# Local attention heads of a hybrid decoder step: the next key is rotated in banks of its own, during the head before

## The chip, the cores and the metric

The kernel runs on one core of one Trainium2 chip. The metric is the device time of one execution in microseconds (us), here the median over several executions. A profiled execution is one such execution, recorded by the hardware profiler; its span is the time from its first to its last recorded instruction. The engines of the core are called TensorE (PE in the rows, its weight loads PEld), VectorE (DVE), ScalarE (ACT), GpSimd (POOL) and SyncE (SP).

## What is computed

One inference step of a four-layer decoder for 512 prompt rows and 8 sample rows, which go through the layers together as 520 columns. The third layer is a sparse attention with 8 heads of 128 dimensions. Cut to what matters:

```python
def dsa_prompt(x, w_in, w_out):
    q, k, v, qi, ki, wi = dsa_project(x, pos, w_in)     # x @ w_in, then rope on q, k, qi, ki
    idx, valid = indexer_topk(qi, wi, ki, pos, n_top)   # 128 keys for each query
    s = einsum('bqhd,bqkhd->bqhk', q, k[idx]) * ATTN_HEAD_DIM ** -0.5
    p = softmax(where(valid, s, -inf))
    o = einsum('bqhk,bqkhd->bqhd', p, v[idx])
    return o @ w_out, k, v, ki                          # rotated keys and values are outputs too
```

The sample rows attend to a paged cache, in a stage after the heads.

## The kernel before

All engines run one program each, ordered by semaphores; a table counts what each stage adds to each semaphore, so that a wait names a semaphore and a count. Matmul operands in f32 are split into a rounded high half and a low half (the difference), and a product is three matmuls: high by high, high by low, low by high.

Weights come in units of 1024 x 128. A unit is loaded by SP into one of four raw slots, ScalarE writes its high half (`split_hi`, line 440), VectorE its low half (`split_lo`, line 450), and TensorE multiplies it with all 520 columns (`multiply`, line 466): 8 chunks of 6 matmuls, 260 columns each. `split_next` (line 458) splits the unit two ahead, once the product that used the same half buffers is done. SP loads the unit four ahead after the low half of a unit is written.

The head stage (`attend`, lines 1032 for ScalarE, 1585 for VectorE, 2148 for TensorE) goes through 8 heads in order, two in each pass of a loop. Each head has a key unit and a value unit. The projection of the next units lies between the softmax steps of a head: four pieces, each ahead of one of the four score tiles. PSUM has eight banks: 0 to 3 hold the projections, 4 to 7 the four score tiles, their transposes, and more:

- rotation of the key: `rotate` (line 2059) multiplies the raw key with an exchange matrix into banks 4 and 5; `d_rotate` (line 1488, three VectorE operations) makes the rotated key from it.
- transposes of the rotated key (bank 6) and of the raw value (bank 7), with their 8 sample rows in banks 4 and 5; ScalarE copies them out (lines 1052 to 1057), GpSimd stores them (lines 715, 717).
- scores of tile t in bank 4 + t; VectorE adds the bias and takes the maximum (line 1650), ScalarE exponentiates (line 1061), VectorE normalises (line 1661); TensorE transposes the weights back into bank 4 + t (line 1821), ScalarE and VectorE split them (lines 1084 and 1722).
- output, four tiles of value products, all in bank 4 (`output`, three matmuls, lines 527 to 529); ScalarE and VectorE write its two halves (lines 1068 and 1667).

In heads 0 to 5 VectorE also does two steps of a top-8 search in each softmax tile (`select`, line 1591), and in head 6 it works out rows of the cache (`find_rows`, line 1605). The stage after the heads (`past`, lines 735, 1070, 1670, 2223) starts gathers from the cache when the last head's line 1667 is done.

In each head ScalarE issues in this order: key copy, split, rounding of the query, value copy, split, rounding of the key (line 1049), the copies of lines 1052 to 1057, four exponentials with the rounding of the transposed weights one tile behind, output. VectorE: low half of weights, query (line 1627), rotation, low half of the key (line 1633), low half of weights, low half of the value (line 1638), four softmax tiles, output. TensorE: rotation, second half of the value's projection, transposes, scores, softmax tiles with projections and value products.

## Time and profile before

| | |
|---|---|
| runs | median 3302.01 us of 3 (3300.86 to 3304.73) |
| profiled execution | 3304.24 us, span 3302.6 us |
| busy, share of the span | TensorE 3095.8 us (94%), weight loads 2918.9 (88%), VectorE 1569.0 (48%), ScalarE 1042.5 (32%), GpSimd 209.5 (6%) |
| chain that ended last | TensorE 87%, VectorE 8%, ScalarE 3%, issue 2% |
| granted TensorE clock | mean 0.957 |
| head stage | about 1604 to 1826 us of the span |

The shares of busy time are averages over stages. The chain is followed back from the last instruction; "issue" is time in which an engine waited for nothing that the profile shows. The granted clock is a share of full speed, and each moment has one of two levels, 1.2 or 2.4 GHz.

### The profile page before, as it was taken

What the parts mean: (1) busy time and instruction counts of PE and PEld (TensorE: products, weight loads), DVE (VectorE), ACT (ScalarE), POOL (GpSimd) and SP (SyncE); (2) the same over time, 40 slices, a digit from 0 to 9 for tenths busy, and PEclk for the clock granted to TensorE, in tenths of its full rate; (3) what the DMA queues carried; (4) which work ended last, traced back from release to release, by engine and by line L of the source; (5) the groups of instructions that cost most, each with busy time, mean ns of one, the idle gap of its engine ahead of it and who ended that gap; (6) DMA issues with size and microseconds to landing.
All of it is one profiled execution on the core that took longest, in us unless ns stands there. A gap on an engine that the chain in (4) does not pass through costs nothing.

```text
span 3302.6 us, 55336 instructions
## 1 busy us (share of the span) xinstructions
PE 3095.8 (94%) x23519; PEld 2918.9 (88%) x23519; DVE 1569.0 (48%) x2426; ACT 1042.5 (32%) x1459; POOL 209.5 (6%) x342
## 2 busy tenths in 40 slices
PE   8999998999976999998887899999999999799997
PEld 7898896999976999986777799999989989699996
DVE  4555555332357332357865453234555555533234
ACT  3333332422234322233333143122523333332223
POOL 0111111000000000010001100000021011000000
PEclk9999998999987999999898899999999999899998
DMA  6344333232311332321122323233344433333231
GB/s 147 131 133 157 128 116 125 77 112 74 98 56 54 89 103 83 96 64 51 52 59 71 116 76 99 84 92 92 94 150 124 146 131 115 109 90 105 75 101 40
DMA packets 491333, 323.14 MB, mean 98 GB/s; under 512 B 29179, under 2 KB 467707, under 8 KB 491130
## 3 DMA queue, kind: packets, MB, share of 16 engines
q1 hardware_dynamic: 464338, 230.14, 24.4%
q0 software_dynamic: 26800, 90.18, 7.9%
q8 instruction: 150, 2.46, 0.3%
q14 instruction: 45, 0.37, 0.0%
HBM read 275.90 MB, written 44.82 MB: 97 GB/s over the span
## 4 chain that ended last, share of the span: by engine, by line
PE 87%; DVE 8%; ACT 3%; issue 2%; DMA 0%; POOL 0%; SPq 0%; ACTq 0%; DVEq 0%; POOLq 0%
PE ps L477 71%; PE ps L1821 2%; PE ps L527 2%; PE ps L529 2%; PE ps L528 2%; PE ps L1951 2%; PE ps L508 2%; PE ps L1941 1%; DVE wf L1537 1%; DVE tiny L1535 1%; DVE wf L1761 1%; DVE wf L1786 1%; DVE w_l L454 1%; PE ps L2309 1%; PE ps L2062 1%
## 5 line engine op out<-in xcount | busy, mean ns | idle before, releaser
L477 PE MATMUL ps<-x_h,w_h 128*128 128x260 f32 x4576 | 942.1, 287 | 8.8 <-DVE w_l L454 6.6
L477 PE MATMUL ps<-x_h,w_l 128*128 128x260 f32 x4576 | 928.4, 285 | 0.0
L477 PE MATMUL ps<-x_l,w_h 128*128 128x260 f32 x4576 | 927.5, 285 | 0.0
L454 DVE TENSOR_TENSOR w_l<-w_raw,w_h 128x1024 fp32r<-128x1024 f32 (+3 forms) x440 | 527.8, 1200 | 796.8 <-ACT w_h L448 796.2
L477 PEld LDWEIGHTS ps<-x_h,w_h 128*128 128x128 f32 x4576 | 715.9, 191 | 32.8 <-issue 23.7
L448 ACT ACTIVATE w_h<-w_raw 128x1024 fp32r<-128x1024 f32 (+3 forms) x440 | 456.0, 1036 | 904.9 <-PE ps L477 874.3
L477 PEld LDWEIGHTS ps<-x_h,w_l 128*128 128x128 f32 x4576 | 712.4, 190 | 0.0
L477 PEld LDWEIGHTS ps<-x_l,w_h 128*128 128x128 f32 x4576 | 712.0, 190 | 0.0
L477 PE MATMUL ps<-rr,w_h 128*128 128x260 f32 x3968 | 639.3, 283 | 2.2 <-DVE w_l L454 1.1
L477 PEld LDWEIGHTS ps<-rr,w_h 128*128 128x128 f32 x3968 | 543.4, 188 | 4.0 <-issue 3.0
L477 PE MATMUL ps<-rr,w_l 128*128 128x260 f32 x1984 | 399.4, 283 | 0.0
L477 PEld LDWEIGHTS ps<-rr,w_l 128*128 128x128 f32 x1984 | 306.7, 189 | 0.0
L1733 DVE TENSOR_TENSOR wf<-ps,wf 128x520 f32<-128x520 f32 x88 | 61.5, 699 | 248.5 <-PE ps L477 248.5
L1091 ACT ACTIVATE wf<-ps 128x520 f32<-128x520 f32 x88 | 53.4, 606 | 337.5 <-PE ps L477 334.6
L527 PE MATMUL ps<-rr 128*128 128x512 f32 (+5 forms) x332 | 121.9, 370 | 18.3 <-DVE rr L1633 10.4
L1821 PE MATMUL ps<-ident,wf 128*128 128x128 f32 (+4 forms) x607 | 95.2, 291 | 32.5 <-DMA wf<-in_x_sample 9.8
L1747 DVE SCALAR_TENSOR_TENSOR x<-x,ps 128x520 f32<-128x520 f32 x40 | 27.8, 696 | 196.1 <-PE ps L477 196.1
L1821 PEld LDWEIGHTS ps<-ident,wf 128*128 128x128 f32 (+4 forms) x607 | 70.5, 142 | 55.7 <-issue 30.8
L529 PE MATMUL ps<-rr 128*128 128x512 f32 (+5 forms) x332 | 116.2, 352 | 0.0
L528 PE MATMUL ps<-rr 128*128 128x512 f32 (+5 forms) x332 | 116.1, 351 | 0.0
L1304 DVE SCALAR_TENSOR_TENSOR wf<-ps,wf 128x512 f32<-128x512 f32 x128 | 89.8, 743 | 17.8 <-PE ps L1942 14.5
L527 PEld LDWEIGHTS ps<-rr 128*128 128x128 f32 (+1 forms) x332 | 64.7, 196 | 35.7 <-issue 19.4
(272 smaller groups left out, 2772.7 us busy)
## 6 DMA issues: line engine op xcount, KB each, us to landing
w_raw<-in_ffn_w_in SPq DMA_DIRECT2D x176, 512.0 KB, 3.8
w_raw<-in_ret_w_in SPq DMA_DIRECT2D x96, 512.0 KB, 4.0
out<-wf POOLq DMA_DIRECT2D x72, 512.0 KB, 3.3
wf<-in_state_ret POOLq DMA_DIRECT2D x64, 512.0 KB, 5.7
w_raw<-in_ffn_w_out SPq DMA_DIRECT2D x32, 768.0 KB, 4.7
w_raw<-in_ffn_w_out SPq DMA_DIRECT2D x32, 640.0 KB, 4.2
w_raw<-in_ret_w_out SPq DMA_DIRECT2D x64, 256.0 KB, 2.9
w_raw<-in_dsa_w_in SPq DMA_DIRECT2D x27, 512.0 KB, 3.9
```

The lines of the kernel that those rows point to most:

```text
L448: C.activation(whole(stage, k, w_h[:, n % 2, 0:m]), landed(stage, k, n, m), ACT.Copy).then_inc(S["w_hi"], 1)
L454: V.tensor_tensor(whole(stage, k, w_l[:, n % 2, 0:m]), landed(stage, k, n, m), whole(stage, k, w_h[:, n % 2, 0:m].bitcast(F32)), ALU.subtr ...
L477: mm = M.matmul(ps[:, 2 * (n % 2) + b, 0:HALF], lhs[:, c, :], rhs[:, c, cols], start=(c == 0 and term == 0), stop=(c == cs - 1 and term == 2))
L508: mm = M.matmul(ps[:, 2 * n + b, 0:HALF], lhs, rhs[:, c, cols], start=(c == 0 and term == 0), stop=(c == DC - 1 and term == 2))
L527: M.matmul(out, lhs_h, rhs_h, start=start, stop=False)
L528: M.matmul(out, lhs_h, rhs_l, start=False, stop=False)
L529: return M.matmul(out, lhs_l, rhs_h, start=False, stop=stop)
L1091: C.activation(halves(sil[:, q]), acc[0], ACT.Silu).then_inc(S["sil"], 1)
L1304: V.scalar_tensor_tensor(st[:, b % 4, d], ps[:, 7, :], k_f[:, d, SEQ + b:SEQ + b + 1], st[:, b % 4, d], ALU.mult, ALU.add).then_inc(S["s_n ...
L1733: V.tensor_tensor(halves(h_raw[:, q]), acc[1], halves(sil[:, q]), ALU.mult).then_inc(S["h_raw"], 1)
L1821: return M.transpose(out, src, ident[0:n, 0:n])
L1951: mm = M.matmul(ps[32 * j:32 * j + 4, 6, :], qz[:, i % 2, d, g, j, :], st[:, (2 * g + j) % 4, d, :], start=(g + d == 0), stop=(g == NB // ...
```

## The change

The loop over passes and halves becomes one loop over heads `g`; all its steps are the same, in another order and with other waits:

- TensorE rotates the key of head g + 1 into banks 5 and 6 (before: 4 and 5), in head g, after the transpose of the fourth weight tile and ahead of the third and fourth value products, once the low half of the third tile is written. Head 0's key is rotated ahead of the loop.
- ScalarE copies the raw key of head g + 1 and splits the next unit behind the third exponential of head g (before: after the output of head g); the query of head g + 1 is rounded behind the fourth weight tile. The rounded key goes ahead of the value copy. The copies of the 8 sample rows go ahead of the large copies of the same bank.
- VectorE splits the low half of that unit ahead of the fourth weight tile's low half, and does the rotation and the query of head g + 1 ahead of the output's low half.
- TensorE's waits follow: the key's transposes no longer wait for the last weight tile, the 8-row key transpose waits for line 1667, the first and second score wait for the 8-row copies alone, the third for the key copy, the fourth for the value's low half, as before.

No operation is added or taken away. The core of the diff:

```diff
@@ ScalarE, attend
+    def key_row(g):
+        at, q = marks.here(stage, g // 2), g % 2
+        act.wait_ge(*at("d_rope", 3 * q))
+        d_copy(at, 0, stage, g // 2, 2 * q, 0)
+        split_next(split_hi, act, stage, g // 2, 2 * q)
+    def query(g):
+        at, q = marks.here(stage, g // 2), g % 2
+        act.wait_ge(*at("s_mm", 4 * q))
+        C.activation(qa_h.rearrange("p (o t) -> p o t", o=1), q_h[:, g:g + 1, :], ACT.Copy).then_inc(S["qa_h"], 1)
+    key_row(0)
+    query(0)
+    for g in range(2 * n):
+        i, q = g // 2, g % 2
+        act.wait_ge(*at("d_rope", 3 * q + 3))
+        act.wait_ge(*at("s_mm", 4 * q))
+        C.activation(ka_h, d_f[:, 0], ACT.Copy).then_inc(S["k_hi"], 1)
+        act.wait_ge(*at("vv_tp", q))
+        d_copy(at, 1, stage, i, 2 * q + 1, 1)
+        split_next(split_hi, act, stage, i, 2 * q + 1)
+        act.wait_ge(*at("kv_out", 64 * q))
+        act.wait_ge(*at("kk_tp", q + 1))
+        C.activation(kvs[0:NB, 0], ps[0:NB, 4, 0:P], ACT.Copy).then_inc(S["kn_cp"], 1)
+        C.activation(kn, view(ps[:, 6], 0, QT, P), ACT.Copy).then_inc(S["kn_cp"], 1)
+        act.wait_ge(*at("vv_tp", q + 1))
+        C.activation(kvs[0:NB, 1], ps[0:NB, 5, 0:P], ACT.Copy).then_inc(S["vn_cp"], 1)
+        C.activation(va_h, view(ps[:, 7], 0, QT, P), ACT.Copy).then_inc(S["vv_hi"], 1)
+        C.activation(vn, view(ps[:, 7], 0, QT, P), ACT.Copy).then_inc(S["vn_cp"], 1)
+        for t in range(QT):
+            w, m = (t + 1) * P, 4 * q + t
+            act.wait_ge(*at("nmx", m + 1))
+            C.activation(pe_[:, t % 2, 0:w], pe_[:, t % 2, 0:w], ACT.Exp, bias=dnm[:, t:t + 1],
+                         accum_out=dsm[:, t:t + 1]).then_inc(S["p_exp"], 1)
+            if t:
+                p_hi(at, m - 1, t - 1)
+            if g < 2 * n - 1 and t == 2:
+                key_row(g + 1)
+        p_hi(at, 4 * q + 3, 3)
+        if g < 2 * n - 1:
+            query(g + 1)
+        act.wait_ge(*at("pv", q + 1))
+        C.activation(o_h[:, g:g + 1, 0:SEQ], ps[:, 4:5, :], ACT.Copy).then_inc(S["o_hi"], 1)
@@ VectorE
-def d_rotate(at, k, tab, slot, to):
+def d_rotate(at, k, tab, slot, to, bank=4):
-    V.tensor_tensor(halves(d_t), ps[:, 4:6, 0:HALF], halves(tab[:, 1]), ALU.mult).then_inc(S["d_rope"], 1)
+    V.tensor_tensor(halves(d_t), ps[:, bank:bank + 2, 0:HALF], halves(tab[:, 1]), ALU.mult).then_inc(S["d_rope"], 1)
@@ VectorE, attend
+    def key_row(g):
+        at, q = marks.here(stage, g // 2), g % 2
+        dve.wait_ge(*at("k_hi", q))
+        dve.wait_ge(*at("kk_tp", q))
+        d_rotate(at, q, dtab, 0, 0, 5)
+    def query(g):
+        at, q = marks.here(stage, g // 2), g % 2
+        dve.wait_ge(*at("qa_h", q + 1))
+        dve.wait_ge(*at("s_mm", 4 * q))
+        V.tensor_copy(qa_l.rearrange("p (o t) -> p o t", o=1), q_l[:, g:g + 1, :].bitcast(F32)
+                      ).then_inc(S["qa_l"], 1)
+    split_next(split_lo, dve, stage, 0, 0)
+    query(0)
+    key_row(0)
+    for g in range(2 * n):
+        i, q = g // 2, g % 2
+        dve.wait_ge(*at("d_rope", 3 * q + 3))
+        V.tensor_copy(ks_d[:, g:g + 1], d_f[:, 0:1, SEQ:T]).then_inc(S["ks_cp"], 1)
+        dve.wait_ge(*at("k_hi", q + 1))
+        V.tensor_tensor(ka_l, d_f[:, 0], ka_h.bitcast(F32), ALU.subtract).then_inc(S["k_lo"], 1)
+        split_next(split_lo, dve, stage, i, 2 * q + 1)
+        dve.wait_ge(*at("d_raw", 2 * q + 2))
+        V.tensor_copy(vs_d[:, g:g + 1], d_raw[:, 1:2, SEQ:T]).then_inc(S["ks_cp"], 1)
+        dve.wait_ge(*at("vn_cp", 2 * q + 2))
...
+        if g < 2 * n - 1:
+            split_next(split_lo, dve, stage, (g + 1) // 2, 2 * ((g + 1) % 2))
+        p_lo(at, 4 * q + 3, 3)
+        if g < 2 * n - 1:
+            key_row(g + 1)
+            query(g + 1)
+        dve.wait_ge(*at("o_hi", q + 1))
+        V.tensor_tensor(o_l[:, g:g + 1, 0:SEQ], ps[:, 4:5, :], o_h[:, g:g + 1, 0:SEQ].bitcast(F32), ALU.subtract
+                        ).then_inc(S["o_lo"], 1)
@@ TensorE
-def rotate(at, k, m, slot):
+def rotate(at, k, m, slot, bank=4):
-        mm = M.matmul(ps[:, 4 + b, 0:HALF], m, d_raw[:, slot, cols], start=True, stop=True)
+        mm = M.matmul(ps[:, bank + b, 0:HALF], m, d_raw[:, slot, cols], start=True, stop=True)
@@ TensorE, attend
+    def key_row(g):
+        at, q = marks.here(stage, g // 2), g % 2
+        pe.wait_ge(*at("d_raw", 2 * q + 1))
+        rotate(at, q, rotm, 0, 5)
+    pe.wait_ge(*late("sc_cp", 0))
+    key_row(0)
+    for g in range(2 * n):
+        i, q = g // 2, g % 2
+        multiply(pe, stage, i, 2 * q + 1, x_h, x_l, DC, range(4, 8))
+        pe.wait_ge(*at("d_rope", 3 * q + 3))
+        for t in range(QT):
+            turn(ps[:, 6, t * P:(t + 1) * P], d_f[:, 0, t * P:(t + 1) * P], P)
+        pe.wait_ge(*at("o_lo", q))
+        turn(ps[0:NB, 4, 0:P], d_f[:, 0, SEQ:T], P).then_inc(S["kk_tp"], 1)
+        pe.wait_ge(*at("d_raw", 2 * q + 2))
+        pe.wait_ge(*at("p_lo", 4 * q))
+        for t in range(QT):
+            turn(ps[:, 7, t * P:(t + 1) * P], d_raw[:, 1, t * P:(t + 1) * P], P)
+        turn(ps[0:NB, 5, 0:P], d_raw[:, 1, SEQ:T], P).then_inc(S["vv_tp"], 1)
+        pe.wait_ge(*at("qa_l", q + 1))
+        pe.wait_ge(*at("k_lo", q + 1))
+        for t in range(QT):
+            w, tile = (t + 1) * P, slice(t * P, (t + 1) * P)
+            if t == 0:
+                pe.wait_ge(*at("kn_cp", 2 * q + 1))
+            elif t == 1:
+                pe.wait_ge(*at("vn_cp", 2 * q + 1))
+            elif t == 2:
+                pe.wait_ge(*at("kn_cp", 2 * q + 2))
+            elif t == 3:
+                pe.wait_ge(*at("vv_lo", q + 1))
+                if g == 6:
+                    pe.wait_ge(*late("row", 10))
+                    turn(ps[:, 7, 0:NB], row, NB).then_inc(S["row_t"], 1)
+                    pe.wait_ge(*late("row_c", 1))
+            three(ps[:, 4 + t, 0:w], qa_h[:, tile], qa_l[:, tile], ka_h[:, 0:w], ka_l[:, 0:w]
+                  ).then_inc(S["s_mm"], 1)
+        for t in range(QT):
+            m = 4 * q + t
+            if g < 2 * n - 1:
+                multiply(pe, stage, (g + 1) // 2, 2 * ((g + 1) % 2) + pieces[t][0], x_h, x_l, DC, pieces[t][1])
+            pe.wait_ge(*at("p_n", m + 1))
+            for j in range(t + 1):
+                mm = turn(ps[:, 4 + t, j * P:(j + 1) * P], pe_[:, t % 2, j * P:(j + 1) * P], P)
+            mm.then_inc(S["p_tp"], 1)
+            if t == 3 and g < 2 * n - 1:
+                pe.wait_ge(*at("p_lo", m))
+                key_row(g + 1)
+            if t:
+                output(at, m - 1, t - 1)
+        output(at, 4 * q + 3, 3).then_inc(S["pv"], 1)
```

## Rows read from the trace of the kernel before

**Rows 1.** Busy time by stretch, head stage: width us, busy (instructions), PEclk, DMA share, GB/s.

```profile
1636.47:1661.55 25.08, 20.91 (x162) 19.51 (x160) 17.80 (x47) 10.63 (x24) 2.57 (x4) 1.00 0.19 51
1661.55:1690.89 29.34, 25.23 (x164) 23.80 (x165) 18.58 (x51) 10.63 (x24) 2.58 (x4) 0.83 0.23 66
...
1773.04:1804.98 31.94, 24.97 (x166) 22.96 (x164) 16.03 (x46) 10.63 (x24) 4.62 (x6) 0.84 0.28 84
1804.98:1824.78 19.80, 15.00 (x70) 13.08 (x69) 9.32 (x30) 8.43 (x21) 2.67 (x4) 0.62 0.19 54
1636.47:1773.04 136.57, 115.86 (x812) 108.73 (x811) 90.90 (x242) 53.16 (x120) 12.88 (x20) 0.90 0.21 59
```

**Rows 2.** Waits, 1628 to 1800 us: engine line <- waited for: us, times, longest.

```profile
PE ps L2062 <- DVE rr L1667: 11.0, 7, 1.6
```

**Rows 3.** Timeline of TensorE: start, us, line, operation [idle before <- releaser].

```profile
1693.90 0.30 PE L527 MATMUL ps<-rr 128*128 128x128 f32 x1 [1.48 <-DVE rr L1633]
...
1694.86 0.39 PE L527 MATMUL ps<-rr 128*128 128x256 f32 x1 [0.44 <-ACT wf L1057]
...
1696.54 0.40 PE L477 MATMUL ps<-x_h,w_h 128*128 128x260 f32 x2
...
1708.86 0.33 PE L527 MATMUL ps<-rr 128*128 128x128 f32 x1 [0.46 <-DVE rr L1722]
...
1710.14 0.28 PE L529 MATMUL ps<-rr 128*128 128x128 f32 x1
1711.98 1.11 PE L2062 MATMUL ps<-wf 128*128 128x260 f32 x4 [1.56 <-DVE rr L1667]
1712.74 0.59 PE L477 MATMUL ps<-x_h,w_h 128*128 128x260 f32 x2
```

**Rows 4.** The same view of ScalarE, 1676 to 1697 us.

```profile
1676.68 0.72 ACT L1061 ACTIVATE wf<-wf,tiny 128x512 f32<-128x512 f32 x1 [1.29 <-DVE tiny L1654]
...
1690.99 0.60 ACT L971 ACTIVATE wf<-ps 128x520 f32<-128x520 f32 x1 [5.74 <-PE ps L477]
1691.49 1.05 ACT L448 ACTIVATE w_h<-w_raw 128x1024 fp32r<-128x1024 f32 x1
1692.44 0.63 ACT L1049 ACTIVATE rr<-wf 128x520 fp32r<-128x520 f32 x1
1692.96 0.59 ACT L1052 ACTIVATE wf<-ps 128x512 f32<-128x512 f32 x1
1693.44 0.25 ACT L1053 ACTIVATE wf<-ps 8x128 f32<-8x128 f32 x1
1693.60 0.57 ACT L1055 ACTIVATE rr<-ps 128x512 fp32r<-128x512 f32 x1
```

**Rows 5.** The same view of VectorE, 1640 to 1697 us.

```profile
1641.10 0.28 DVE L1650 CUSTOM_DVE_ANT_0 wf<-ps,wf 128x128 f32<-128x128 f32 x1
...
1651.89 0.55 DVE L1722 TENSOR_TENSOR rr<-ps,rr 128x384 fp32r<-128x384 f32 x1
...
1680.29 0.69 DVE L1722 TENSOR_TENSOR rr<-ps,rr 128x512 fp32r<-128x512 f32 x1 [1.15 <-ACT rr L1084]
...
1684.75 1.23 DVE L454 TENSOR_TENSOR w_l<-w_raw,w_h 128x1024 fp32r<-128x1024 f32 x1 [0.75 <-ACT w_h L448]
1685.89 0.42 DVE L1627 CAST rr<-rr 128x520 fp32r<-128x520 f32 x1
1686.26 0.70 DVE L1492 TENSOR_TENSOR wf<-ps,wf 128x520 f32<-128x520 f32 x1
...
1688.34 0.17 DVE L1631 COPY wf<-wf 128x8 f32<-128x8 f32 x1
...
1694.92 0.68 DVE L1638 TENSOR_TENSOR rr<-ps,rr 128x512 fp32r<-128x512 f32 x1
```

**Rows 6.** The same view of TensorE, at the first hand-over.

```profile
1629.89 2.07 PE L2062 MATMUL ps<-wf 128*128 128x260 f32 x4 [1.56 <-DVE rr L1667]
1631.40 1.00 PE L477 MATMUL ps<-x_h,w_h 128*128 128x260 f32 x2
```

More of the change, by code:

```diff
@@ new lines, in attend @@
+                split_next(split_lo, dve, stage, 0, 0)
[3 more added lines that the diff above has]
+                    i, q = g // 2, g % 2
+                    at = marks.here(stage, i)
+                    dve.wait_ge(*at("d_rope", 3 * q + 3))
[6 more added lines that the diff above has]
+                    dve.wait_ge(*at("vn_cp", 2 * q + 2))
+                    V.tensor_tensor(va_l, view(ps[:, 7], 0, QT, P), va_h.bitcast(F32), ALU.subtract
+                                    ).then_inc(S["vv_lo"], 1)
+                    if g == 6:
+                        find_rows()
+                        dve.wait_ge(*late("row_t", 1))
+                        V.tensor_copy(rows.bitcast(U32), ps[:, 7, 0:NB]).then_inc(S["row_c"], 1)
+                    for t in range(QT):
+                        w, m, to = (t + 1) * P, 4 * q + t, BIAS_AT[t]
+                        dve.wait_ge(*at("s_mm", m + 1))
+                        if t >= 2:
+                            dve.wait_ge(*at("p_tp", m - 1))
+                        carry(dve)
+                        V.tensor_tensor_reduce(out=pe_[:, t % 2, 0:w], in0=ps[:, 4 + t, 0:w], in1=bias[:, to:to + w],
+                                               scale=ASCALE, scalar=-3.0e38, op0=ALU.add, op1=ALU.max,
+                                               accum_out=dmx[:, t:t + 1]).then_inc(S["s_sc"], 1)
+                        dve.wait_ge(*at("s_sc", m + 1))
+                        V.tensor_scalar(dnm[:, t:t + 1], dmx[:, t:t + 1], -1.0, None, ALU.mult).then_inc(S["nmx"], 1)
+                        if g < 6:
+                            select(2 * (4 * g + t))
+                            select(2 * (4 * g + t) + 1)
+                        dve.wait_ge(*at("p_exp", m + 1))
+                        V.reciprocal(drc[:, t:t + 1], dsm[:, t:t + 1]).then_inc(S["p_rc"], 1)
+                        dve.wait_ge(*at("p_rc", m + 1))
+                        V.tensor_scalar(pe_[:, t % 2, 0:w], pe_[:, t % 2, 0:w], drc[:, t:t + 1], None, ALU.mult
+                                        ).then_inc(S["p_n"], 1)
+                        if t:
+                            p_lo(at, m - 1, t - 1)
+                    if g < 2 * n - 1:
[7 more added lines that the diff above has]
+                                    ).then_inc(S["o_lo"], 1)
@@ new lines, in key_row @@
+                def key_row(g):
[6 more added lines that the diff above has]
+                    i, q = g // 2, g % 2
+                    at = marks.here(stage, i)
+                    multiply(pe, stage, i, 2 * q + 1, x_h, x_l, DC, range(4, 8))
[21 more added lines that the diff above has]
+                            pe.wait_ge(*at("vv_lo", q + 1))
+                            if g == 6:
+                                pe.wait_ge(*late("row", 10))
[3 more added lines that the diff above has]
+                              ).then_inc(S["s_mm"], 1)
+                    for t in range(QT):
+                        m = 4 * q + t
[8 more added lines that the diff above has]
+                            key_row(g + 1)
+                        if t:
+                            output(at, m - 1, t - 1)
+                    output(at, 4 * q + 3, 3).then_inc(S["pv"], 1)
```

125 lines of the change are left out of this document (removed).

## The prediction

> **What bounds the kernel now.** I read three views of the head stage (lines 1032, 1585 and 2148), about 1604 to 1826 us of the span. First the busy time by stretch [rows 1], cut at the end of each head's V product; I call that moment M. A head takes 25.08 us where TensorE's granted clock is 1.00 throughout, and 29.34 us where it is 0.83; the two kinds alternate, and five heads take 136.57 us at a mean of 0.90. TensorE is busy 20.91 of 25.08 us, VectorE 17.80, ScalarE 10.63: TensorE is the bound, but it stands still some 4 us a head, and then runs partly at 1.2 GHz. Second, the list of what TensorE waits for [rows 2]: the largest item is the rotation's matmul (line 2062) waiting for the low half of the previous head's output (line 1667), 1.6 us at every one of seven hand-overs. Third, the same waits in order of time for one head at full clock [rows 3]: 1.48 us before the first score, for the low half of the key (line 1633), 0.44 before the second, 0.46 inside the value products, 1.56 before the rotation. ScalarE's rows [rows 4] say why the scores wait: V copy, weight rounding, key rounding, key copy and value copies stand one behind the other from M + 0.10.
>
> **The change, part by part.** All at full clock, from rows 3 to 5, M = 1690.89.
>
> *Rotation in banks 5 and 6, ahead of the last two value products.* Now the rotation writes banks 4 and 5, and bank 4 holds the output, so it must wait until the output is read. The last output matmul is issued at 1710.14; the next could follow 0.11 later, as within the products, at 1710.25. From there to the start of the V product at 1712.74 pass 2.49 us [rows 3]. With the rotation gone from there, the V product follows at once: -2.49. The rotation itself is not saved; it costs 1712.74 - 1711.98 = +0.76 between the fourth transpose and the third product. There it fills the time in which the fourth product waits for its low half: the 0.46 us wait with some 0.15 us of restart, -0.6. Net -2.33 a hand-over. It needs the K copy (ScalarE, after the third exponential) and the low half of tile 2; both end before the fourth transpose.
>
> *K copy and weight split behind the third exponential.* ScalarE issues the pair in 1692.44 - 1690.99 = 1.45 us [rows 4]. It moves into a stretch where ScalarE stood idle 1.29 us before the fourth exponential [rows 4], so that exponential can be later by 0.2 us; were nothing idle, by 1.45. I take 0 for TensorE, since VectorE has two top-8 steps to do meanwhile, and TensorE has no wait for the normalised weights (line 1661) in the steady heads; cover gone, it is 0.2 a head. On VectorE the weights' low half goes ahead of the last tile's low half, where VectorE idles 1.15 us [rows 5]; the subtraction issues in 1685.89 - 1684.75 = 1.14. 0. The loads on SP's queue follow the low half, so they start earlier; none was waited for. The POOL queue keeps its order.
>
> *Rotation on VectorE ahead of the output's low half.* Three operations, 1688.34 - 1686.26 = 2.08 us, and the query cast, 0.37 us [rows 5], now stand between the last low half and line 1667. Behind them wait the key's transposes (after the V product, 3.07 us long) and the 8-row transpose into bank 4. I follow VectorE from M: value low half done at 4.0 (below); the four softmax tiles take 1651.89 + 0.55 - 1641.10 = 11.3, to 15.3; split and last low half to 17.2, rotated key at 19.3, output's low half at about 20.3. The next M is at 22.0. So 1.7 to 2.7 us are spare, and the cost is 0; if the spare is used up, every further us is one a head.
>
> *Key rounded ahead of the value copy, small copies first.* The key is ready long before M, so its rounding leaves the chain behind M. Then, with issue times of [rows 4], the 8-row key copy goes at M + 1.55 where the rounding stood, the key copy at 1.70, the 8-row value copy at 2.18, value rounding at 2.33, value copy (as long as the key copy) at 2.81, done at 3.4. The value's low half (0.60 us, line 1638) ends at 4.0 instead of 4.63 (1694.92 + 0.60) [rows 5], and the fourth score, which waits for it, releases the next projection at M + 4.9 instead of 1696.54 - 1690.89 = 5.65 [rows 3]: -0.75. In these 4.9 us TensorE has four short waits, none over 0.7 us by the same times.
>
> A rule stands against stopping there. TensorE's busy row counts 20.91 us in the full-clock head, its weight-load row 19.51 [rows 1]. The Trainium skill (Perfetto Trace Analysis, Identifying the Most-Contended Engine) says that matmul busy time is no good measure of TensorE's headroom and that the weight loads' busy share is a good one. By that rule a head could shrink to an estimated 19.5 us, and the time would be some 12 us lower than mine. No row shows work that would fill those last waits, so the sum stays with the waits that the edits remove.
>
> **The sum.** A full-clock head: 25.08 - 2.33 - 0.75 = 22.0. Five heads: 136.57 - 110 = 26.6 if all run at full clock. What the clock keeps costing is not shown, so I bound it: nothing at best; at worst as much as now, 136.57 - 5 x 25.1 = 11.1 us. In the trace the clock fell to 1.2 GHz after the 1.56 us stop before the rotation, or after the 1.48 and 0.44 us stops in the scores; the longest stop left is about 0.7 us. I take 2.5 us, near the lower end. The first hand-over ran at 1.2: rotation 1.51 us and V product 1636.47 - 1631.40 = 5.07 [rows 6] instead of 0.76 and 3.07, so it gives 2.33 + 2.75 = 5.1. The last (inside 31.94 us at 0.84 [rows 1]) gives 2.33, 0.75 for the score chain, through which the row search starts earlier, and 0 to 2.75 for the clock; I take 1.4: 4.5. The eighth head (19.80 us) has no projections under it and follows the ScalarE and VectorE chain: 0.7. Sum: 26.6 - 2.5 + 5.1 + 4.5 + 0.7 = 34.4 us. The stage after the heads starts its gathers on the last line 1667, so all of it moves to the end. The profiled execution took 3304.24 us: 3269.8. It stands 2.2 us over the median of 3302.01, so the prediction for a median is 3268.
>
> **Rivals.**
> (1) The clock gains nothing: the shorter waits still let it fall as often. For it: a third of the time of every second head is at 1.2 GHz although no stop there exceeds 1.6 us [rows 1, 3]. Against: the large stops go. Gain 26.6 - 11.1 + 2.3 + 3.1 + 0.7 = 21.6: about 3280.
> (2) VectorE becomes the bound. It is busy 17.80 us in a head of 25.08 [rows 1] and would be in one of 22.0, with rotation and cast in series ahead of line 1667. If its waits on ScalarE (1.15 and 2 to 3 us more in a head) stay where they are, it overruns its spare by some 1.6 us: 5 x 1.6 = 8 us back, 3276.
> (3) Slower: TensorE stays at 1.2 GHz through the heads. Place: the stretch from M to the fourth score, now transposes and short scores with four stops. Of the 22.0 us, 16.9 are matmul; at half speed throughout a head would take 38.9 instead of 27.3, seven hand-overs +81 us: 3383. It decides from 10.6 us at 1.2 GHz in a head (5.3 us lost). For it: the eighth head, without wide projections, has 0.62 over 19.80 us [rows 1]. Against: each steady head has wide projections for over half its time, during which the clock came back in the trace.
> (4) The edits do nothing that counts: the wait before the rotation only moves to the 8-row transpose into bank 4, which now waits for line 1667. For it, that line comes 0.1 us later; against, 3.07 us of V product lie before it. 3302, within the bound.
>
> **How the numbers follow.** Forecast 0.70, rival 1 0.15, rival 2 0.08, rival 3 0.03, rival 4 0.04. A measurement of this kernel tells 0.2% (6.6 us) from no change. Forecast and rivals 1 and 2 are faster by more: 0.93; rival 4 the same: 0.04; rival 3 slower: 0.03. The best case has no fall of the clock left and a full 2.75 at the last hand-over, 38.3 us: 3264; a few us more if later stages keep the clock better. The other end takes in rivals 1 and 2 with both their bounds: 3284. Range 3260 to 3284.
>
> **What would show it.** Right: M to M of 22 to 23 us, granted clock near 1.00 in these stretches, no wait of line 2062 for line 1667, the first score waiting for the 8-row key copy and the fourth for line 1638, V product directly behind the value products. Wrong: a new wait of TensorE for the rotated key or for line 1661, stretches with 0.83 as often as now, or a time over 3284.

## The result, and the profile after

The changed kernel takes 3270.47 us, the median of 4 runs (3267.33 to 3272.78), the kernel before 3303.37 (3300.86 to 3308.75, 4 runs): a ratio of 0.9899, 95% interval 0.9887 to 0.9911. The profiled execution took 3270.22 us, its span is 3268.5 us (before: 3304.24 and 3302.6), and the mean granted clock rose from 0.957 to 0.962. The time was predicted at 3268. That it came so close is luck: two errors of the prediction cancel in it, as the stages show.

The head stage by stretch, from M to M as in [rows 1]: width, busy time (instructions) of TensorE, its weight loads, VectorE, ScalarE and GpSimd, then PEclk, DMA share, GB/s. The first line is one head; the lines behind the mark are the sum of five heads, then head 6 and head 7.

```profile
1629.73:1651.73 22.00, 20.82 (x165) 19.57 (x163) 18.08 (x48) 10.53 (x24) 2.58 (x4) 1.00 0.26 73
...
1629.73:1739.73 110.00, 104.07 (x813) 97.78 (x811) 90.22 (x242) 52.65 (x120) 12.90 (x20) 1.00 0.25 73
1739.73:1766.91 27.18, 23.06 (x166) 21.58 (x164) 15.70 (x46) 10.53 (x24) 4.62 (x6) 0.87 0.32 98
1766.91:1786.06 19.15, 13.94 (x70) 11.93 (x68) 8.82 (x29) 7.91 (x20) 2.67 (x4) 0.72 0.18 55
```

The alternation of [rows 1] is gone: each of five heads takes 22.00 us at a granted clock of 1.00, 110.00 us where there were 136.57. TensorE's busy time in a full-clock head is as before (20.82 us beside 20.91); only its idle time went. Of the 26.57 us that the five heads give, 14.78 are idle time of TensorE and 11.79 busy time, which was longer at the lower clock (115.86 us busy before, 104.07 after).

What TensorE waits for, 1628 to 1770 us, answers to [rows 2]: us in total, times, longest.

```profile
PE ps L1849 <- DVE wf L1630: 3.2, 1, 3.2
PE ps L527 <- ACT wf L1060: 2.9, 7, 0.4
PE ps L527 <- DVE rr L1661: 2.7, 5, 0.5
PE ps L1849 <- ACT wf L971: 1.5, 7, 0.2
PE ps L527 <- DVE wf L1666: 0.3, 1, 0.3
```

The 11.0 us ahead of the rotation are gone, and the rotation (now line 2090) is in no wait. What is left per head is 0.21, 0.42 and 0.54 us, on the copies and on the value's low half behind M. The 3.2 us are the row search of head 6.

TensorE in order of time, one head, which answers to [rows 3]:

```profile
1645.03 0.60 PE L1849 MATMUL ps<-ident,wf 128*128 128x128 f32 x4
1645.46 1.04 PE L2090 MATMUL ps<-wf 128*128 128x260 f32 x4
1646.15 0.41 PE L527 MATMUL ps<-rr 128*128 128x128 f32 x1
...
1648.53 0.28 PE L529 MATMUL ps<-rr 128*128 128x128 f32 x1
1648.64 0.46 PE L477 MATMUL ps<-x_h,w_h 128*128 128x260 f32 x2
...
1653.67 0.30 PE L527 MATMUL ps<-rr 128*128 128x128 f32 x1 [0.42 <-ACT wf L1060]
...
1655.90 0.50 PE L527 MATMUL ps<-rr 128*128 128x512 f32 x1 [0.54 <-DVE rr L1661]
...
1656.70 0.40 PE L477 MATMUL ps<-x_h,w_h 128*128 128x260 f32 x2
```

The rotation takes 1646.15 - 1645.46 = 0.69 us between the fourth transpose and the third product. The V product starts 0.11 us behind the last value product, where 2.60 us lay (1712.74 - 1710.14 in [rows 3]). From M (1651.73) to the next projection piece pass 4.97 us, where 5.65 passed.

ScalarE in the same head, which answers to [rows 4]: key copy and split run where it stood idle, and the exponential (line 1069) follows without a gap.

```profile
1641.28 0.60 ACT L971 ACTIVATE wf<-ps 128x520 f32<-128x520 f32 x1
1641.77 1.06 ACT L448 ACTIVATE w_h<-w_raw 128x1024 fp32r<-128x1024 f32 x1
1642.71 0.72 ACT L1069 ACTIVATE wf<-wf,tiny 128x512 f32<-128x512 f32 x1
```

The last head's output comes 38.7 us earlier than before, yet the end only 34.0 us (3304.24 - 3270.22). The other 4.7 us are lost in stages that the change does not touch. One piece of them lies in the cache stage, first before, then after:

```profile
1844.78:1869.10 24.32, 18.98 (x52) 7.33 (x52) 4.43 (x12) 0.49 (x2) 2.33 (x3) 0.86 0.24 74
```

```profile
1806.06:1832.06 26.00, 20.38 (x52) 8.32 (x52) 4.71 (x12) 0.49 (x2) 2.64 (x3) 0.77 0.25 79
```

The same 52 matmuls take 1.7 us more, at 0.77 in place of 0.86.

### The profile page after: what moved, and what is told of

Same layout as the page of the kernel before. It is cut to its first block, busy times and chain, and to the rows that moved or that the text cites. A ratio compares the mean times of both kernels' runs of the same rounds, so it can differ in the third digit from the quotient of the medians.

```text
span 3268.5 us, 55344 instructions
## 1 busy us (share of the span) xinstructions
PE 3081.4 (94%) x23519; PEld 2905.9 (89%) x23519; DVE 1568.0 (48%) x2426; ACT 1041.5 (32%) x1459; POOL 209.6 (6%) x342
## 4 chain that ended last, share of the span: by engine, by line
PE 88%; DVE 7%; ACT 3%; issue 2%; DMA 0%; POOL 0%; SPq 0%; ACTq 0%; DVEq 0%; POOLq 0%
PE ps L477 71%; PE ps L1849 2%; PE ps L527 2%; PE ps L528 2%; PE ps L529 2%; PE ps L1979 2%; PE ps L508 2%; PE ps L1969 1%; DVE wf L1548 1%; DVE wf L1789 1%; DVE tiny L1546 1%; DVE wf L1814 1%; DVE w_l L454 1%; ACT w_h L448 1%; PE ps L2346 1%
## 5 line engine op out<-in xcount | busy, mean ns | idle before, releaser
L477 PEld LDWEIGHTS ps<-x_h,w_h 128*128 128x128 f32 x4576 | 710.6, 190 | 32.2 <-issue 23.7
L1849 PE MATMUL ps<-ident,wf 128*128 128x128 f32 (+4 forms) x607 | 95.3, 290 | 34.6 <-DMA wf<-in_x_sample 9.9
L1849 PEld LDWEIGHTS ps<-ident,wf 128*128 128x128 f32 (+4 forms) x607 | 70.3, 142 | 57.9 <-issue 31.5
L527 PEld LDWEIGHTS ps<-rr 128*128 128x128 f32 (+1 forms) x332 | 64.1, 194 | 26.0 <-issue 11.9
```

The costliest lines, as they stand in the source:

```text
L477: mm = M.matmul(ps[:, 2 * (n % 2) + b, 0:HALF], lhs[:, c, :], rhs[:, c, cols], start=(c == 0 and term == 0), stop=(c == cs - 1 and term == 2))
L527: M.matmul(out, lhs_h, rhs_h, start=start, stop=False)
L1849: return M.transpose(out, src, ident[0:n, 0:n])
```

## The experiments

Each run leaves a profile. Five heads are measured from one output copy to the sixth; by that measure they take 136.60 us at a clock of 0.90 before and 110.00 at 1.00 after. The lead is how much earlier than in the profile of before a point is reached.

**1. The score chain undone.** In the changed kernel ScalarE rounds the key behind the value copy again, the large copies go first, and scores 0 and 1 wait for both copies of their pair.

```diff
-act.wait_ge(*at("d_rope", 3 * q + 3))
-act.wait_ge(*at("s_mm", 4 * q))
-C.activation(ka_h, d_f[:, 0], ACT.Copy).then_inc(S["k_hi"], 1)
 act.wait_ge(*at("vv_tp", q))
 d_copy(at, 1, stage, i, 2 * q + 1, 1)
 split_next(split_hi, act, stage, i, 2 * q + 1)
+act.wait_ge(*at("d_rope", 3 * q + 3))
+act.wait_ge(*at("s_mm", 4 * q))
+C.activation(ka_h, d_f[:, 0], ACT.Copy).then_inc(S["k_hi"], 1)
...
-    pe.wait_ge(*at("kn_cp", 2 * q + 1))
+    pe.wait_ge(*at("kn_cp", 2 * q + 2))
```

> The changed kernel with one part undone: ScalarE rounds the rotated key behind the value copy and its split again, and the first two score tiles wait for both copies of their pair again. Theory (each stop on the way from the last value product to the scores is worth its length): the five heads between heads 1 and 6 go from 22.00 to about 22.75 us each, seven hand-overs together cost about 5 us, 3275 to 3276 us against 3270 for the changed kernel; TensorE shows stops of about 1.0 us or more ahead of the first score tile. Rival 1 (it was the order on ScalarE that held the clock in the heads): the clock of the five heads falls below 0.95 and they take 24 us or more, 3280 us or above. Rival 2 (the score chain is hidden behind the K and V transposes): heads stay at 22.0 us, 3270 us.

Measured: 3279.25 us, ratio to before 0.9918 (0.9900 to 0.9935). Its five heads, then the waits that came back, then three stretches of 2 us in one head:

```profile
1627.24:1747.38 120.14, 109.51 (x813) 104.12 (x812) 90.28 (x243) 52.62 (x120) 12.87 (x20) 0.93 0.24 67
...
1680.60:1682.60 2.00, 0.55 (x4) 0.44 (x4) 1.79 (x3) 1.92 (x6) 0.59 (x1) 0.89 0.00 0
1682.60:1684.60 2.00, 2.00 (x7) 2.00 (x8) 1.93 (x9) 0.49 (x2) 1.99 (x4) 0.50 0.60 139
1684.60:1686.60 2.00, 2.00 (x12) 1.73 (x12) 1.93 (x8) 0.56 (x2) 0.00 (x0) 0.76 1.12 342
```

```profile
PE ps L527 <- DVE rr L1656: 8.9, 6, 1.5
PE ps L527 <- ACT wf L1065: 2.6, 6, 0.4
```

Rival 1, in the heads: 24.03 us each, at 0.93, and some 9 us in all. Behind the stop of 1.5 us, in which TensorE was busy 0.55 of 2 us, it runs at 1.2 GHz (0.50) through the scores that follow and into the next pieces. Of the 2.03 us a head that this part gives, 0.94 are more idle time (10.63 us in five heads, 5.93 in the changed kernel) and 1.09 longer busy time (109.51 us, 104.07), at the clock that falls behind the stop.

**2. The wait for the output's low half put back**, ahead of the V product:

```diff
+pe.wait_ge(*at("o_lo", q))
 multiply(pe, stage, i, 2 * q + 1, x_h, x_l, DC, range(4, 8))
```

> The changed kernel with one wait added: TensorE starts the second half of a head's V projection only when VectorE has written the low half of the previous head's output, which is the wait that stood ahead of the rotation before. Theory: a stop of 1.5 to 1.7 us comes back at each of seven hand-overs, from 0; at full clock a head takes 23.5 to 23.7 us, 11 to 12 us in all, 3281 to 3282 us. Rival 1 (this stop alone also lowers the granted clock, which was 0.83 to 1.00 in the heads before): the five heads show under 0.95 and take 25 us or more, 3290 us or above. Rival 2 (the stop is given back, since what follows was waiting for ScalarE and VectorE anyway): under 0.5 us a head, 3273 us or less.

Measured: 3282.38 us (0.9928, 0.9911 to 0.9944). Five heads:

```profile
1625.34:1746.19 120.85, 107.86 (x812) 100.87 (x811) 90.27 (x243) 52.59 (x120) 12.87 (x20) 0.97 0.23 67
```

For most heads the theory's mechanism: behind a stop of 1.41 us three take 23.61 to 23.62 us at 1.00, that is 1.61 more than 22.00. The other two take 25.12 and 24.88 at 0.93, as rival 1 had it for all five. So a stop at this place cost somewhat more than its length in all five heads, and the clock too in two. That the time is the theory's is partly luck: the last head's output comes 14.8 us later than in the changed kernel, and part of that comes back behind the heads (experiment 8).

**3. The rotation behind the last value product**, its own banks kept:

```diff
-if t == 3 and g < 2 * n - 1:
-    pe.wait_ge(*at("p_lo", m))
-    key_row(g + 1)
 if t:
     output(at, m - 1, t - 1)
...
 output(at, 4 * q + 3, 3).then_inc(S["pv"], 1)
+if g < 2 * n - 1:
+    key_row(g + 1)
```

> The changed kernel with TensorE's rotation of the next key behind the last value product of a head instead of ahead of the values of tile 2; its own banks are kept. Theory: the rotation then lies on the path between the last value product and VectorE's rotated key. Two matmuls cost about 0.6 us, and the rotated key (2.0 us of VectorE work) and its rounding come 2.8 us later than now, while V's second half takes about 2.9 us of TensorE: the K transposes wait little, 22.0 us a head become 22.6 to 23.5, 3274 to 3281 us. Rival (the banks alone do it, VectorE and ScalarE have spare time): 0.0 to 0.2 us a head, 3270 to 3271 us. Rival 2 (the place among the value products is what carries the gain): over 2.0 us a head, 3285 us or more.

Measured: 3269.00 us (0.9888, 0.9870 to 0.9905). Five heads and the wait that came back inside the products:

```profile
1626.27:1739.81 113.54, 105.66 (x812) 98.25 (x812) 90.17 (x242) 53.10 (x120) 12.88 (x20) 1.00 0.25 71
```

```profile
PE ps L527 <- DVE rr L1750: 2.3, 5, 0.5
```

In the heads the theory: 22.67 us or a little more each, at full clock; the place inside the products is worth 0.67 us a head, because the rotation fills the wait of 0.46 us. In the total the rival: no slower than the changed kernel. The last head's output comes 4.2 us later than in the changed kernel, and the end does not; experiment 8 takes this up.

**4. VectorE's rotation behind the output's low half:**

```diff
-if g < 2 * n - 1:
-    key_row(g + 1)
-    query(g + 1)
 dve.wait_ge(*at("o_hi", q + 1))
 V.tensor_tensor(o_l[:, g:g + 1, 0:SEQ], ...).then_inc(S["o_lo"], 1)
+if g < 2 * n - 1:
+    key_row(g + 1)
+    query(g + 1)
```

> The changed kernel with VectorE's three rotation operations and the next query's low half behind the subtraction for the output's low half instead of ahead of it. Theory: output's low half comes as early as ScalarE's copy lets it (ScalarE starts it 0.2 us behind the last value product), the rotated key about 3 us later than now, close to where the V product's second half ends; the K transposes wait 0.3 to 0.6 us a head, 3272 to 3275 us. Rival (VectorE has enough spare time that the order is worth nothing): heads stay at 22.0 us, 3270 us. Rival 2 (late query and key push the score tiles as well): over 1.0 us a head, 3278 us or more.

Measured: 3272.44 us (0.9896, 0.9879 to 0.9913), the time that the theory said, but too close to the changed kernel's 3270.47 to be told from it. The heads tell: 114.90 us for five, four of them 22.79 to 22.82 us, and one 23.66 us at a clock of 0.93. TensorE, line 1849, in one head:

```profile
1699.56 0.76 PE L1849 MATMUL ps<-ident,wf 128*128 128x128 f32 x5 [0.43 <-DVE wf L1506]
1700.72 0.77 PE L1849 MATMUL ps<-ident,wf 128*128 128x128 f32 x5 [0.40 <-ACT wf L971]
```

The key's transposes wait 0.43 us for the rotated key, and the value's 0.40 for the copy, 0.2 more than in the changed kernel. VectorE's order is worth 0.8 us a head, more than the 0.3 to 0.6 said: the rotated key ends 0.37 us behind M (1699.50 against 1699.13), where the changed kernel has it 2.6 us ahead of M, so the other order uses up the spare time.

**5. Key copy and split behind the fourth weight tile:**

```diff
-        if g < 2 * n - 1 and t == 2:
-            key_row(g + 1)
     p_hi(at, 4 * q + 3, 3)
     if g < 2 * n - 1:
+        key_row(g + 1)
         query(g + 1)
```

> The changed kernel with one part undone in the order of ScalarE: the next key's copy and the split of its weights stand behind the fourth weight tile instead of behind the third exponential. Theory: the copy then ends about 1.3 us behind the point at which TensorE wants to rotate, and VectorE's low half of the split, with the fourth weight tile's low half queued behind it, comes about 2.5 us later; a head goes from 22.0 to 24.0 to 24.8 us, 14 to 20 us in all without a loss of clock, 3284 to 3290 us. Rival 1 (the place is free, ScalarE being busy for 10.5 us of 22): under 0.3 us a head, 3272 us or less. Rival 2 (only the rotation's own wait counts, VectorE takes up the rest): 1.3 us a head, 3278 to 3281 us.

Measured: 3282.56 us (0.9923, 0.9906 to 0.9940). Five heads, and the new waits:

```profile
1630.31:1752.04 121.73, 106.22 (x813) 98.19 (x812) 90.12 (x243) 53.15 (x120) 12.88 (x20) 1.00 0.23 66
```

```profile
PE ps L2089 <- ACT wf L971: 6.4, 5, 1.3
PE ps L527 <- DVE rr L1749: 3.9, 6, 0.6
```

The theory in the heads: 24.35 us each (24.0 to 24.8 said), the rotation waiting 1.27 us for the raw key and the last product 0.65 for its low half. At the last head's output 17.5 us are lost, 1.3 of them ahead of the heads already; at the end the medians differ by 12.1, under the theory's 14 to 20, and experiment 8 shows where the rest comes back. So with own banks but without the early key copy, TensorE stops at the rotation all the same. The clock stays at 1.00, although the stops of a head (1.27 + 0.65 + 0.21 + 0.42 + 0.54 = 3.1 us) are longer than those of experiment 1 (1.48 + 0.44 + 0.21 = 2.1 us), which lowered it in every head.

**6. Own banks alone, in the kernel before:**

```diff
-pe.wait_ge(*at("o_lo", q))
-rotate(at, q, rotm, 0)
+pe.wait_ge(*late("sc_cp", 0))
+rotate(at, q, rotm, 0, 5)
...
+pe.wait_ge(*at("o_lo", q))
 turn(ps[0:NB, 4, 0:P], d_f[:, 0, SEQ:T], P).then_inc(S["kk_tp"], 1)
```

> The kernel before with one part of the change alone: the rotation writes two banks that the value products do not use, so that it no longer waits for the low half of the output, which is waited for at the 8-row transpose instead. ScalarE's key copy stays behind the output's copy. Theory: the rotation then waits for the raw key, which ScalarE copies right behind the output's copy (0.5 us later), so that only about 0.4 to 0.5 us of the stop of 11.0 / 7 = 1.57 us go; 3 to 4 us in all at the same clock, 3297 to 3304 us beside 3301 to 3311 of the kernel before. Rival (the banks are what the gain comes from): the stop is gone, 1.5 us a head and 11 us, with the clock up by some hundredths, 3290 us or less.

Measured: 3300.80 us (0.9986, 0.9977 to 0.9996). Its waits and five heads:

```profile
PE ps L527 <- DVE rr L1633: 7.1, 5, 1.5
PE ps L2062 <- ACT wf L971: 5.0, 4, 1.2
```

```profile
1625.15:1761.88 136.73, 117.59 (x811) 110.12 (x810) 90.84 (x242) 53.17 (x120) 12.88 (x20) 0.89 0.21 59
```

The theory, for the wait: the rotation now waits 1.24 us for ScalarE's key copy, in place of 1.56 for the output's low half. But the five heads take 136.73 us, as long as before (136.60), so the 0.3 us that each stop gave do not show even there.

**7. The score chain alone, in the kernel before**, the rotation untouched:

```diff
+act.wait_ge(*at("d_rope", 3 * q + 3))
+C.activation(ka_h, d_f[:, 0], ACT.Copy).then_inc(S["k_hi"], 1)
 act.wait_ge(*at("vv_tp", q))
 d_copy(at, 1, stage, i, 2 * q + 1, 1)
 split_next(split_hi, act, stage, i, 2 * q + 1)
-act.wait_ge(*at("d_rope", 3 * q + 3))
-C.activation(ka_h, d_f[:, 0], ACT.Copy).then_inc(S["k_hi"], 1)
...
-    pe.wait_ge(*at("kn_cp", 2 * q + 2))
+    pe.wait_ge(*at("kn_cp", 2 * q + 1))
```

> The kernel before with the other part of the change alone: ScalarE rounds the rotated key ahead of the value copy, copies the 8-row blocks first and releases the score tiles one by one; the rotation stays where it was, with its stop of 1.56 us. The run that undid this part in the changed kernel cost 8 us, 24.0 us a head in place of 22.0, where the part's own stop is 0.75 us: the clock fell to 0.93 in every head behind a stop of 1.48 us ahead of the first score tile. Theory (that stop, in a stretch of short transposes, is what makes the clock fall; the stop ahead of the rotation mostly does not, as the run with that stop put back showed 1.00 in four heads of five): the five heads show 24.3 to 25.0 us each at a clock of 0.97 to 1.00 in most of them, 121 to 126 us where the kernel before took 136.6; 3286 to 3295 us beside 3301 to 3310. Rival 1 (each stop is worth its length alone): 0.75 us a head, the clock between 0.83 and 1.00 from head to head as before, 3299 to 3303 us. Rival 2 (only both stops gone bring the clock back): the heads keep their mean clock of 0.90 or fall lower, 3300 us or above.

Measured: 3301.38 us (0.9990, 0.9981 to 0.9999). Five heads:

```profile
1622.56:1753.57 131.01, 114.58 (x811) 106.07 (x810) 91.62 (x242) 53.63 (x120) 12.87 (x20) 0.92 0.21 61
```

My theory fell. The stop ahead of the first score is gone (0.42 us instead of 1.48), but the clock falls in four heads of five (0.87 to 0.93). In one of them the rotation, behind its stop of 1.56 us, takes 2.07 us in place of 1.11; the fifth head stays at 1.00 with a stop of 1.57 us ahead of its rotation. The time lies in the range of rival 1 and in that of rival 2, and does not tell them apart. The theory also leaned on a misreading: in experiment 2 three heads of five stayed at 1.00, not four. In the heads the score chain alone is worth more than its time says: the five take 5.6 us less than before, and the last output comes 10.7 us earlier, counted from the norm ahead of the heads, but most of that is lost behind the heads (experiment 8). Score chain alone (5.6) and everything but the score chain (16.5, experiment 1) make 22.1 of the 26.6 us that the whole change gives in five heads. At the end the two give 0.10% and 0.82%, together 0.92% beside 1.01%, a difference smaller than these intervals. Own banks alone and the score chain alone are not the two halves of the change: the early key copy, VectorE's order and the place of TensorE's rotation are in neither.

**8. What becomes of a gain behind the heads.** The changed kernel ran twice more, and so did those of experiments 3 and 9.

> The changed kernel once more, unaltered, beside the kernel of the next run. Theory: the five heads show 22.00 us each at a clock of 1.00 again, since nothing in them depends on the run, while the stages behind the heads, which the change does not touch, move by up to about 2 us each from profile to profile, as they did in the four profiles of the other experiments (the gain at the end of the heads and the gain at the next norm differed by -1.9, -1.8, -0.1, +0.9 and -1.8 us); median 3268 to 3273 us. Rival: the 4.6 us that the first profile of the changed kernel lost between the end of the heads and the end of the program are a lasting cost of the change, and the same 1.9 and 2.3 us are lost in the same two stages again.

> The changed kernel a third time, beside the next two on one chip, to settle what becomes of a gain behind the heads. So far two profiles of it lost 4.7 and 7.4 us of their lead between the last head's output and the end of the program. Theory (the stages behind the heads take one of a few lengths, some 2 us apart, by where TensorE's clock falls in them, in any kernel): the loss is again between 0 and 8 us and differs from the two before; median 3268 to 3272 us. Rival (a lasting loss that belongs to the changed kernel): 4.7 to 7.4 us are lost once more, and the same 1.9 us between the heads and the next norm.

> The kernel with TensorE's rotation behind the last value product once more. Its heads took 22.67 us and its last head's output came 4.2 us later than in the changed kernel, yet its median was 3269.0 against 3270.5 and 3270.9. Theory (lengths of the later stages vary from run to run in both): heads of 22.67 us again, median 2 to 4 us above that of the run before this one. Rival (its later stages are steadily quicker, so that the 0.67 us a head cost nothing in the end): median equal to the run before this one or below it, by up to 2 us, and again no loss behind the heads.

Measured: the changed kernel 3270.85 (0.9887, 0.9871 to 0.9904) and 3270.70 (0.9897, 0.9880 to 0.9913); with the rotation last 3268.16 (0.9896, 0.9879 to 0.9912). The lead at five points (the norm ahead of the heads, the last output copy, the next norm, the norms at 2870 and 3267 us of before):

| kernel | ahead | last output | next norm | norm at 2870 | norm at 3267 |
|---|---|---|---|---|---|
| changed, three profiles | -0.1, 1.0, 1.7 | 38.7, 39.6, 40.6 | 36.8, 37.7, 38.6 | 34.0, 34.7, 35.6 | 34.0, 32.2, 33.1 |
| rotation last, two | 0.6, 0.9 | 34.5, 35.3 | 34.4, 35.1 | 34.5, 35.1 | 34.5, 35.1 |
| value split late, two | 1.3, 1.7 | 43.8, 44.4 | 41.7, 42.2 | 38.6, 39.1 | 36.0, 36.6 |
| score chain undone (1) | 1.2 | 26.1 | 24.3 | 25.1 | 25.1 |
| wait put back (2) | 1.2 | 23.9 | 24.8 | 21.7 | 21.7 |
| VectorE's order (4) | -0.3 | 31.5 | 29.7 | 30.5 | 30.5 |
| key copy late (5) | -1.4 | 21.2 | 22.2 | 19.1 | 19.1 |
| own banks alone (6) | 2.9 | 6.4 | 6.5 | 6.1 | 3.7 |
| score chain alone (7) | 1.2 | 11.9 | 10.1 | 7.0 | 4.5 |

The rivals, and not my theory: the changed kernel loses 1.9 to 2.0 us of its lead up to the next norm and 2.8 to 3.1 up to the one at 2870 in each profile, with the rotation last at most 0.2 is lost. Only the last stretch differs between profiles of the changed kernel (0.0, 2.5, 2.5).

The loss is no property of the changed kernel, though. The stage from the last output copy to the next norm, the same 583 matmuls each time, in the kernel before, the changed kernel, and experiments 7 and 5:

```profile
1824.06:1920.34 96.28, 86.18 (x583) 73.13 (x582) 47.46 (x62) 13.83 (x22) 14.01 (x15) 0.93 0.38 121
```

```profile
1785.34:1883.52 98.18, 88.32 (x583) 74.88 (x583) 47.44 (x62) 13.84 (x22) 14.01 (x15) 0.89 0.37 119
```

```profile
1812.19:1910.28 98.09, 88.23 (x583) 74.81 (x582) 47.45 (x62) 13.83 (x21) 14.00 (x15) 0.89 0.37 119
```

```profile
1802.89:1898.15 95.26, 85.15 (x583) 72.41 (x583) 47.47 (x62) 13.83 (x21) 13.98 (x15) 0.94 0.38 122
```

In all fourteen profiles it takes one of three lengths, and the granted clock goes with the length: 98.1 to 98.5 us at 0.89 (the changed kernel, experiments 1, 4, 7 and 9), 96.2 to 96.5 at 0.93 (the kernel before, experiment 6, and the rotation last), 95.3 to 95.4 at 0.94 (experiments 2 and 5). A late or an early start does not decide it: the changed kernel enters the stage at 1785 us, experiment 7 at 1812.

Another place is the norm at 2317 us of before and the start of the layer behind it. Stretches of 3 us, first of the third profile of the changed kernel, then of the second with the rotation last, which does the same work some 2.8 us later:

```profile
2279.00:2282.00 3.00, 3.00 (x28) 2.97 (x27) 2.60 (x6) 1.30 (x2) 0.00 (x0) 1.00 0.00 0
2282.00:2285.00 3.00, 2.85 (x15) 2.56 (x14) 2.38 (x6) 0.21 (x1) 0.00 (x0) 0.55 0.00 0
2285.00:2288.00 3.00, 3.00 (x16) 3.00 (x15) 2.09 (x4) 1.36 (x2) 0.00 (x0) 0.50 0.60 175
```

```profile
2285.00:2288.00 3.00, 2.61 (x23) 2.41 (x22) 2.66 (x6) 0.21 (x1) 0.00 (x0) 1.00 0.00 0
2288.00:2291.00 3.00, 1.78 (x13) 1.41 (x12) 3.00 (x6) 2.76 (x4) 0.00 (x0) 1.00 0.62 180
...
2294.00:2297.00 3.00, 2.39 (x11) 2.40 (x12) 2.58 (x5) 2.94 (x5) 0.00 (x0) 0.50 0.00 0
```

The clock falls in both, but in the one during the norm, when TensorE had been busy throughout, in the other some 8 us further on in the same work. So the fall comes at another point of the same work. The time at which the work starts does not set the point: the profiles of the changed kernel reach this norm up to 1.7 us apart and lose the same, and the second with the rotation last reaches it only 1.0 us after the latest of them and loses nothing. What sets it was not found.

**9. One more step of the same kind: V's split behind the copies.** ScalarE splits V's weights last, VectorE's low half of it goes into the second score tile, and two search steps go ahead in its place.

```diff
-split_next(split_hi, act, stage, i, 2 * q + 1)
 act.wait_ge(*at("kv_out", 64 * q))
...
 C.activation(vn, view(ps[:, 7], 0, QT, P), ACT.Copy).then_inc(S["vn_cp"], 1)
+split_next(split_hi, act, stage, i, 2 * q + 1)
...
-split_next(split_lo, dve, stage, i, 2 * q + 1)
+if g < 6:
+    select(8 * g)
+    select(8 * g + 1)
...
+if t == 1:
+    split_next(split_lo, dve, stage, i, 2 * q + 1)
+elif g < 6:
+    op = 8 * g + 2 * (t + (t == 0))
```

> The changed kernel with one more step of the same kind: ScalarE splits V's weights behind the six value and key copies instead of ahead of them, and VectorE's low half of that split moves into the second score tile, in whose place two row-search operations go ahead of the low half of V. Theory: the two waits that are left at a hand-over, 0.42 us of the first score tile and 0.54 us of the fourth, go; five heads of 22.00 us become 21.0 to 21.3 us at full clock; 3264 to 3266 us against 3270. Rival 1 (the row search and split crowd VectorE in the first tiles and the wait goes to the normalisation of tiles 1 and 2): heads stay at 22.0 us or more, 3270 us or above. Rival 2 (weights split later hold up the projection pieces of the next head): TensorE waits for the weights' low half appear at the second projection piece, 22.5 us or more a head, 3273 us or above.

> The kernel with V's weight split behind the value copies once more, beside the changed kernel. Theory: heads of 21.37 us again, and a median 3 to 5 us below that of the changed kernel in the same call, 3264 to 3268 us. Rival (the gain of 0.64 us a head is lost in the stages behind): within 1 us of the changed kernel.

Measured: 3267.01 us (0.9877, 0.9860 to 0.9893) and 3268.04 (0.9896, 0.9879 to 0.9912). Five heads and the waits:

```profile
1625.32:1732.15 106.83, 102.73 (x813) 97.67 (x812) 90.74 (x243) 53.45 (x120) 12.92 (x20) 1.00 0.27 75
```

```profile
PE ps L1854 <- DVE wf L1630: 3.3, 1, 3.3
PE ps L527 <- DVE rr L1663: 2.7, 5, 0.5
PE ps L1854 <- ACT wf L971: 1.2, 6, 0.2
```

A head takes 21.37 us, 0.63 less; the theory said 21.0 to 21.3, and its first time, 3264 to 3266 us, was too low as well. The wait of the first score is gone; that of the fourth, which I had thought to remove too, is as long as before, because the low half still waits for the value copy. The last output comes 3.6 to 4.1 us earlier than in the changed kernel's three profiles, counted from the norm ahead of the heads. Over the runs of both the medians are 3267.9 of 8 and 3270.7 of 12: 2.8 us, less than the 0.2% that a measurement tells. Beside the kernels that ran with it, it was the fastest both times, by little.

## Why the prediction was right, and where it was not

- **Rotation in own banks, ahead of the last two products.** Said: -2.33 us a hand-over, no wait of its own. The new order does it: V product 0.11 us behind the products, 0.69 us for the rotation (0.76 said), no wait of line 2090. The term holds only together: banks alone take 0.32 us off the stop and nothing off the five heads (experiment 6); in the changed kernel the place inside the products carries 0.67 (experiment 3) and the early key copy 2.35 (experiment 5).
- **Key copy and split behind the third exponential: 0** for TensorE. Right; no wait on the exponential's side appeared.
- **VectorE: 0, with 1.7 to 2.7 us to spare.** Right. The rotated key ends at 1649.13, 19.4 us behind M (19.3 said), 2.6 us ahead of the next M, and the output's low half at 1650.16, 1.6 ahead of it. Experiment 4 shows that the order is needed: the other way round costs 0.8 us.
- **Score chain: -0.75.** The way from M to the next piece measures 4.97 us, 0.68 less than before, as the sum had it. What it is worth in the changed kernel is more, 2.03 us a head in experiment 1, because the clock falls behind that stop; in the kernel before it is 1.1 us (experiment 7). The sum had the clock as a term of its own, so this is no error of the total; but the two do not separate.
- **A full-clock head of 22.0.** Measured 22.00.
- **The clock's cost in five heads: 2.5 us taken, bounds 0 to 11.1.** Mis-sized: it measures 0. The reason that I gave, that the longest stop left is about 0.7 us, stands beside a measured 0.54. But length alone is not the rule: 1.41 us lowered the clock in two heads of experiment 2, and 1.57 us left one head of experiment 7 at 1.00. So the reason for a small term is not shown.
- **First hand-over 5.1.** From the output copy of head 0 to M it gives 5.16 (8.04 before, 2.88 after), as said. But M comes 6.74 us earlier (1629.73 against 1636.47): the other 1.58 lie in head 0 itself, ahead of its output, and the sum had no term for them. Last hand-over 4.5: 31.94 to 27.18, so 4.8. Eighth head 0.7: 19.80 to 19.15, so 0.65.
- **"All of it moves to the end."** This step failed. The heads gave 26.57 + 6.74 + 4.76 + 0.65 = 38.7 us, against 34.4 said, and 4.7 of it were lost behind, in stages whose work is the same: 1.9 up to the next norm, where the granted clock is 0.89 in place of 0.93, and 2.8 from there to the norm at 2870, where the clock falls at another point. Why it falls there stays open. The two errors, 4.3 and 4.7, cancel.
- **The rule on weight loads.** It made a head of an estimated 19.5 us, from the weight-load row. That row did not move: 19.51 before, 19.57 after, and 97.67 / 5 = 19.53 in experiment 9. The Trainium skill (Perfetto Trace Analysis, Identifying the Most-Contended Engine) judges TensorE's headroom by the share of peak FLOPs and by the weight loads' busy share, and not by matmul busy time. The trace agrees in so far as the busy row was no floor: with one more order of ScalarE it fell from 20.82 us a head to 20.55 (102.73 / 5). That order's gain of 0.63 us would have fitted under either row, so it does not decide between them. No run here shows that the remaining 1.8 us, from 21.37 to the row of 19.5, can be had.
- **Rivals.** VectorE as the bound, the moved wait and a head at 1.2 GHz throughout: none is in the trace. That the clock gains nothing: the reverse, in five heads, though part of what it gave there was lost behind them.

## What to carry to other kernels

A chain across three engines gives way only when all its links are moved. The stop ahead of the rotation stayed at 1.24 us with own banks alone, and the five heads as long as before; and with own banks but the key copied late it came back at 1.27 us. Price such a change by the whole chain at full clock, and keep the clock's share as a range of its own. And do not carry a gain in one stage straight to the end: compare the leads at later landmarks, with a second profile, and set the parts of a change against each other inside the stage that they touch, before a difference of a few us is put down to an edit.

## What the runs showed of the hardware

- The granted clock does not follow the sum or the longest of a head's stops alone. With 1.48 and 0.44 us around the first two scores it fell in every head (experiment 1), with 1.27 and 0.65 at the rotation and the last product in none (experiment 5), with 1.41 ahead of the V product in two of five (experiment 2); and one head of experiment 7 kept 1.00 with 1.57 ahead of its rotation. What decides among these was not settled.
- Stages with the same work repeat their length to within some 0.3 us for one kernel, and differ by 2 to 3 us between kernels: 1.9 to 2.0 us up to the next norm and 2.8 to 3.1 from there to the norm at 2870 are lost in each of three profiles of the changed kernel, and at most 0.2 in two with the rotation last. The last stretch, with 0.0 in one profile of the changed kernel and 2.5 in two, is the exception.
- The stage behind the heads took 98.1 to 98.5, 96.2 to 96.5 or 95.3 to 95.4 us, at granted clocks of 0.89, 0.93 and 0.94, for the same 583 matmuls, in fourteen profiles that entered it between 1780 and 1824 us. Profiles of one kernel always had the same length, wherever they entered; what chooses among the three was not found.
